# Hybrid encoder trunk: the seams between stages, the order of cross attention, and chunk attention's transposes and first scores between the products of v

## The reference

```python
mem_n = rms_norm(mem, mem_norm_g)                       # 256 memory rows
for layer in range(2):
    if layer == 0:   # S5 heads and gated DeltaNet heads, then one output projection "abo"
        x = x + concat([a_out, b_out]) @ ab_w_out
    else:            # 16 heads of 64; a chunk of 64 sees itself and 8 chunks back, with a bias
        q, k, v = split(rms_norm(x, c_norm_g) @ c_w_qkv) ; q, k = rms_norm(q), rms_norm(k)
        x = x + (softmax(q @ k.T * scale + bias) @ v) @ c_w_out
    # cross attention, 4 heads of 256, into the 256 memory rows
    q = rms_norm(rms_norm(x, xa_norm_g) @ w_q) ; k, v = split(mem_n @ w_kv) ; k = rms_norm(k)
    x = x + (softmax(q @ k.T / 16) @ v) @ w_out
    h = rms_norm(x, f_norm_g)
    x = x + (silu(h @ w_gate) * (h @ w_up)) @ w_down    # 2816 hidden
```

## Time and profile before

| | |
|---|---|
| median of 3 runs | 1712.14 us (1711.04 to 1712.47) |
| the profiled execution | 1712.62 us, its span 1710.8 us |
| PE busy | 1644.2 us, 96% of the span |
| DVE, ACT, POOL busy | 766.8, 627.0, 228.7 us |
| TensorE clock granted, mean | 0.99 |

### The profile page before, as it was taken

The page is one execution under the profiler, slowest core; times in us unless marked ns, Lnnn a source line. Parts: engine busy times, 40 slices in busy tenths (PEclk is TensorE's granted clock), DMA queues, the critical chain, the costliest instruction groups (busy, mean ns, idle before and its releaser), DMA issues.

```text
span 1710.8 us, 22110 instructions
## 1 busy us (share of the span) xinstructions
PE 1644.2 (96%) x9102; PEld 1337.5 (78%) x9102; DVE 766.8 (45%) x996; ACT 627.0 (37%) x1022; POOL 228.7 (13%) x309
## 2 busy tenths in 40 slices
PE   5999999899899999999999998899989999999999
PEld 4788787778678888888888885588767788888887
DVE  4669345544524444442244438734353444444222
ACT  6543433444515222221133336824451422222110
POOL 3863233010001111110000000000000011111000
PEclk9998999999999999999999998999999999999999
DMA  6612012242022333332222321225302143333221
GB/s 204 134 50 74 2 53 75 86 161 98 30 69 74 98 98 98 98 98 98 99 87 86 99 99 50 75 74 169 102 25 75 53 119 95 94 92 95 92 98 74
DMA packets 146799, 151.82 MB, mean 89 GB/s; under 512 B 8864, under 2 KB 109344, under 8 KB 146592
## 3 DMA queue, kind: packets, MB, share of 16 engines
q1 hardware_dynamic: 146720, 150.69, 29.0%
HBM read 147.53 MB, written 3.15 MB: 88 GB/s over the span
## 4 chain that ended last, share of the span: by engine, by line
PE 91%; DVE 4%; ACT 3%; issue 1%; DMA 0%; POOL 0%; SPq 0%; ACTq 0%; DVEq 0%
PE ps L325 25%; PE ps L327 25%; PE ps L326 25%; PE ps L1679 2%; PE ps L1656 1%; PE ps L2016 1%; PE ps L2028 1%; PE ps L959 1%; PE ps L2038 1%; PE ps L417 1%; PE ps L1274 1%; PE ps L889 1%; ACT w_hi L293 1%; PE ps L1079 1%; PE ps L1363 1%
## 5 line engine op out<-in xcount | busy, mean ns | idle before, releaser
L325 PE MATMUL ps<-h_hi,w_hi 128*128 128x512 f32 x864 | 338.1, 391 | 4.2 <-DVE w_lo L1849 3.9
L326 PE MATMUL ps<-h_lo,w_hi 128*128 128x512 f32 x864 | 336.7, 390 | 0.0
L297 DVE TENSOR_TENSOR w_lo<-raw,w_hi 128x2048 fp32r<-128x2048 f32 x70 | 160.5, 2292 | 389.8 <-ACT w_hi L293 389.8
L293 ACT ACTIVATE w_hi<-raw 128x2048 fp32r<-128x2048 f32 x84 | 160.8, 1916 | 423.6 <-PE ps L327 423.0
L327 PE MATMUL ps<-h_hi,w_lo 128*128 128x512 f32 x704 | 274.4, 390 | 0.0
L325 PEld LDWEIGHTS ps<-h_hi,w_hi 128*128 128x128 f32 x864 | 162.6, 188 | 38.8 <-issue 5.3
L326 PEld LDWEIGHTS ps<-h_lo,w_hi 128*128 128x128 f32 x864 | 162.7, 188 | 33.3
L1849 DVE TENSOR_TENSOR w_lo<-raw,w_hi 128x2048 fp32r<-128x2048 f32 x44 | 138.1, 3139 | 53.5 <-ACT w_hi L1831 53.5
L327 PEld LDWEIGHTS ps<-h_hi,w_lo 128*128 128x128 f32 x704 | 132.5, 188 | 27.8
L1831 ACT ACTIVATE w_hi<-raw 128x2048 fp32r<-128x2048 f32 x44 | 84.3, 1916 | 161.1 <-PE ps L327 161.1
L325 PE MATMUL ps<-w_hi,a_hi 128*128 128x512 f32 x352 | 137.3, 390 | 1.7 <-DVE up L1847 1.7
(11 more groups left out here) (372 smaller groups left out, 2639.2 us busy)
## 6 DMA issues: line engine op xcount, KB each, us to landing
raw<-in_f_w_gate SPq DMA_DIRECT2D x44, 512.0 KB, 4.0
raw<-in_f_w_up SPq DMA_DIRECT2D x44, 512.0 KB, 5.2
raw<-in_f_w_down SPq DMA_DIRECT2D x44, 512.0 KB, 4.4
raw<-in_xa_w_kv SPq DMA_DIRECT2D x16, 1024.0 KB, 5.0
raw<-in_c_w_qkv SPq DMA_DIRECT2D x12, 1024.0 KB, 5.1
raw<-in_ab_w_in SPq DMA_DIRECT2D x10, 1024.0 KB, 5.9
raw<-in_xa_w_q SPq DMA_DIRECT2D x8, 1024.0 KB, 5.0
raw<-in_xa_w_out SPq DMA_DIRECT2D x8, 1024.0 KB, 5.0
```

The costliest lines, as they stand in the source:

```text
L293: a.activation(w_hi[:, n % 2, :], raw[n % 2], ACT.Copy).then_inc(sem("w_hi"), 1)
L297: v.tensor_tensor(w_lo(n)[:, n % 2, :], raw[n % 2], w_hi[:, n % 2, :].bitcast(F32), ALU.subtract).then_inc(sem("w_lo"), 1)
L325: pe.matmul(out, a[0], b[0], start=start, stop=False)
L326: pe.matmul(out, a[0], b[1], start=False, stop=False)
```

## The change

- The normalised memory's transposes move between the two halves of abo1. They use four banks for the eight blocks (`norm_bank`), so a block of 256 columns shares a bank with another; ACT writes the second four after DVE has done with the first. PE then waits for all eight low parts and goes on to kv without waiting for the last additions to x.
- The first four transposed blocks of x move between the halves of kv's last projection, the other four between the halves of xq's first; ACT and DVE write them there.
- Cross attention: ACT loads the table of the exponential ahead of k's blocks; PE transposes q's blocks 0 to 3, does head 0's scores, transposes blocks 4 to 7, does head 1's scores. Head 0's scores wait for k's and for q's first two blocks alone. DVE rescales a head before it takes the maxima of a later one.
- FFN up: the first turn of ACT's and DVE's loops is written out, with the weights of block 2 split ahead of SiLU and of the gated product.
- Chunk attention: v's first projection has q's and k's 16 transposed blocks between its tiles (banks 4 to 7), v's second the scores of pairs 0 and 1 (banks 0 to 3). ACT and DVE write the blocks, v's rows and the first exponentials between pieces; piece ca4_1 moves behind k's last row tile and piece cao0_1 into the turn m = 6. The probabilities of pairs 0 and 1 lie elsewhere in memory.

The diff, cut to its core:

```diff
+        def norm_bank(n, k):
+            banks = KT * n // TT
+            return ps[:, k % banks, k // banks * n * P:(k // banks + 1) * n * P]
...
-        def rows_pe(pe, t, name, srcT, tiles, bank, ready=None, bank_free=None, between=None, mid=None):
+        def rows_pe(pe, t, name, srcT, tiles, bank, ready=None, bank_free=None, between=None, mid=None, step=None):
...
+                    if step is not None:
+                        step(kh, i)
...
+            def x_between():
+                pe.wait_ge(sem(f"{t}_k"), after(f"{t}_k", 4))
+                turn_rows_pe(pe, f"x{l}", 0, "co_x" if l else "mo_x")
...
+            pe.wait_ge(sem(f"{t}_q"), after(f"{t}_q", 8))
+            xq_turn_pe(pe, l, range(0, 4))
...
+            exp_table(a)
             kv_turned_act(a, l)
...
             maxes(0)
+            xq_turned_dve(v, l, (5, 7))
+            rescale(0)
             maxes(1)
-            rescale(0)
             turned(0)
...
                     turned(h + 1)
-                if h + 3 < XH:
-                    maxes(h + 3)
                 if h + 2 < XH:
                     rescale(h + 2)
                 out_lo(h)
+                if h + 3 < XH:
+                    maxes(h + 3)
...
             xa_scores_pe(pe, l, 0)
+            xq_turn_pe(pe, l, range(4, KT))
             xa_scores_pe(pe, l, 1)
...
+            weights_hi(0, 0)
+            silu(0, 0)
+            silu(0, 1)
+            weights_hi(0, 1)
+            with a.Fori(1, FT // 2) as j:
...
+            gate(0, 0)
+            weights_lo(0, 0)
+            gated(0, 0)
+            gate(0, 1)
+            gated(0, 1)
+            weights_lo(0, 1)
+            with v.Fori(1, FT // 2) as j:
...
+                        step={4: step_turn, 5: step_scores}.get(p))
+        CA_TURNS = ((), range(0, 3), range(3, 6), range(6, 8), range(8, 10), range(10, 12), range(12, 14), range(14, 16))
+        CA_FIRST = ((), ((0, CA_ROWS[0:3]),), ((0, CA_ROWS[3:4]),), (), ((1, CA_ROWS[0:3]),), ((1, CA_ROWS[3:4]),), (), ())
...
+            pieces_hi(a, "ca4_1")
+            for t in (0, 2, 4):
+                ca_turned(a, t)
+            pieces_hi(a, "ca5_0")
+            for t, values in ((6, ()), (8, (16,)), (10, (17,)), (12, (18, 19)), (14, ())):
+                ca_turned(a, t)
+                for n in values:
+                    ca_value_rows(a, n)
+            pieces_hi(a, "ca5_1")
+            pieces_hi(a, "ca5_1", 1)
+            a.wait_ge(sem("c_max"), 1)
+            for e in range(2):
+                for i in CA_EXP:
+                    ca_exp(a, 0, e, i)
+            for n in range(20, 24):
+                ca_value_rows(a, n)
...
+            if t < 4:
+                pe.wait_ge(sem("c_rows"), 13 + t)
+            else:
+                pe.wait_ge(sem(f"c_T{'av'[t % 2]}"), after(f"c_T{'av'[t % 2]}", (t - 4) // 2 + 1))
...
-            ca_scores_pe(pe, 0)
-            ca_scores_pe(pe, 1)
+            pe.wait_ge(sem("c_v"), 8)
...
+                if m == CH // 2 - 2:
+                    pieces_hi(a, "ca5_1", 2)
...
-            rows_pe(pe, "mo", "abo1", cat, TT, 4)
-            pe.wait_ge(sem("mo_x"), after("mo_x", 8))
-            norm_pe(pe, "m", mem_x, mem_x)
+            rows_pe(pe, "mo", "abo1", cat, TT, 4, between=mem_between)
+            ready_T(pe, "m", KT - 1)
```

More of the change, by code:

```diff
@@ L438, in sqrt_table, with exp_table @@
             a.wait_ge(sem("act_warm"), count[name])
+        def exp_table(a):
+            a.activation(warm, pcol("one"), ACT.Exp).then_inc(sem("act_warm"), 1)
+            name = "act_warm"
+            count[name] = count.get(name, 0) + 1
+            a.wait_ge(sem("act_warm"), count[name])
         def squares_act(a, t, x, junk, dst, ready=None, halves=(0, 1)):
@@ L1626, in xq_act @@
                 a.wait_ge(sem(f"{t}_turned"), after(f"{t}_turned", k + 1))
-                a.activation(qT[:, k, :], ps[:, (k + 4) % 8, :], ACT.Copy, scale=pcol(f"xq_g{l}", 0)).then_inc(sem(f"{t}_qTa"), 1)
+                a.activation(qT[:, k, :], ps[:, 4 + k % 4, :], ACT.Copy, scale=pcol(f"xq_g{l}", 0)).then_inc(sem(f"{t}_qTa"), 1)
         def xq_dve(v, l):
@@ L1649, in xa_scores_pe @@
             if h < 2:
-                for k in range(6) if h == 0 else range(6, KT):
+                if h == 0:
+                    pe.wait_ge(sem(f"kv{l}_kTa"), after(f"kv{l}_kTa", 4))
+                    pe.wait_ge(sem(f"kv{l}_kTv"), after(f"kv{l}_kTv", 4))
+                for k in (2 * h, 2 * h + 1):
                     pe.wait_ge(sem(f"xq{l}_qT{'av'[k % 2]}"), after(f"xq{l}_qT{'av'[k % 2]}", k // 2 + 1))
@@ L1662, in xa_turn_pe @@
             pe.wait_ge(sem(f"{t}_p"), after(f"{t}_p", h + 1))
+            if h == 0:
+                for e in "av":
+                    pe.wait_ge(sem(f"xq{l}_qT{e}"), after(f"xq{l}_qT{e}", 4))
             if h > 0:
@@ L1940, in bank_free, with turned_free, step_turn, step_scores @@
                     pe.wait_ge(sem("c_rows"), n - 7)
+            def turned_free(n):
+                for t in range(n - 8, n - 7):
+                    pe.wait_ge(sem(f"c_T{'av'[t % 2]}"), after(f"c_T{'av'[t % 2]}", t // 2 + 1))
+            def step_turn(kh, i):
+                for t in CA_TURNS[4 * kh + i]:
+                    ca_turn_pe(pe, t)
+            def step_scores(kh, i):
+                for m, rows in CA_FIRST[4 * kh + i]:
+                    ca_scores_pe(pe, m, rows)
             for p in range(6):
@@ L2086, in exp @@
             def exp(m, e, i):
-                p = p_c(m, e, i)
-                a.activation(p, p, ACT.Exp, bias=c_neg[:, m % 2, e, i:i + 1], accum_out=c_sum[:, m % 2, e, i:i + 1]).then_inc(sem("c_exp"), 1)
-            a.wait_ge(sem("c_max"), 1)
-            for e in range(2):
-                for i in CA_EXP:
-                    exp(0, e, i)
+                if (m, e) != (1, 0):
+                    ca_exp(a, m, e, i)
             for m in range(CH // 2):
@@ L2285, in _ @@
                 kv_pe(pe, l)
-                pe.wait_ge(sem(f"kv{l}_k"), after(f"kv{l}_k", 4))
-                pe.wait_ge(sem(f"kv{l}_v"), after(f"kv{l}_v", 4))
-                for half in range(2):
-                    turn_rows_pe(pe, f"x{l}", half, "co_x" if l else "mo_x")
                 xq_pe(pe, l)
@@ L2376, in _ @@
                 pieces_hi(a, f"kv{l}3_1", 2)
-                for half in range(2):
-                    turned_hi_act(a, f"x{l}", f"xa_g{l}", half)
+                turned_hi_act(a, f"x{l}", f"xa_g{l}", 1)
                 xq_act(a, l)
@@ L2460, in _ @@
                 kv_dve(v, l)
+                turned_lo_dve(v, f"x{l}", f"xa_g{l}", 0)
                 pieces_lo(v, f"kv{l}3_1", 2)
-                for half in range(2):
-                    turned_lo_dve(v, f"x{l}", f"xa_g{l}", half)
+                turned_lo_dve(v, f"x{l}", f"xa_g{l}", 1)
                 xq_dve(v, l)
```

179 lines of the change are left out of this document (104 added, 75 removed).

## The result

The median after the change is 1683.12 us (1680.52 to 1684.19, 4 runs), beside 1711.59 us (1710.72 to 1712.47, 4 runs) of the kernel before: ratio 0.9831, 95% interval 0.9814 to 0.9848, 28.5 us less. The prediction was 1681.5 us. The profiled execution took 1684.19 us, with a span of 1682.4.

What follows compares the result with a forecast made beforehand. PE, busy 96% of the span, was taken to bound the kernel, so only its standing or slow running could be won. Terms 3.7 + 3.5 + 8.8 + 4.8 + 9.8 = 30.6 us gave 1681.5 us, range 1675 to 1690.

Steps and rivals of the forecast that it cites:

- the likeliest case: Whole kernel: the forecast's own sum holds, 1681.5 us, with a range of 1676 to 1687 and a chance of 0.60.
- A, memory's seam: Layer 0, abo1 to kv: moving memory's transposes between abo1's halves removes PE's standing around them, saving 3.7 us.
- B, x's seam: kv and xq, both layers: x's transposes between projection halves leave 0.4 us of standing, saving 1.75 us a layer, 3.5 in all.
- C, cross attention: Both layers: rescaling waits and a clock fall go, two new waits come; 7.4 becomes 3.05 us, saving 4.4 a layer, 8.8 in all.
- D, FFN's start: Start of FFN up, both layers: earlier split shortens PE's wait for block 2's low part to 0.45 us, saving 4.8 us.
- E, chunk attention: Transposes and first scores between v's products win 11.4 us, less 1.6 for the moved piece: 9.8 us saved.
- the last values start 1.6 us later: End of chunk attention's loop: piece cao0_1 in turn m = 6 delays DVE's copy of the last pair's probabilities, costing 1.6 us.
- in turns 0 to 5 the piece would have been hidden: Chunk attention's loop: piece cao0_1 would be covered in turns 0 to 5, but nothing covers it in turn m = 6.
- wait for evacuations in v's first projection: Rival, chunk attention: PE stands for every pair because blocks are written out late, 8 us, giving 1689.5; chance 0.17.
- The seams' waits: Rival: standing removed in A, B and D returns at the next piece, losing 12.0 us, giving 1693.5; chance 0.05.
- The clock kept falling: Rival: clock falls behind remaining waits in cross attention, FFN and the loop's start, 5.4 us in all, giving 1687; chance 0.15.
- The slower case: Rival: transposes between v's products keep the clock at half there, 35 us for 192 matmuls, giving 1716.5; chance 0.03.

Runs made afterwards that it cites:

- Experiment 11: Kernel after the change, with x's second four blocks transposed behind the second tile of xq's first half: 1682.5 us.
- Experiment 2: Kernel after the change, with cross attention's order put back as before: 1695.94 us.
- Experiment 5: Kernel after the change, with ACT's and DVE's halves of piece cao0_1 moved behind the loop of chunk attention: 1680.47 us.
- experiment 7: Kernel after the change, with piece cao0_1 in turn m = 2 instead of 6 on both engines: 1683.52 us.
- experiments 3 and 4: Kernel after the change with one part put back each: 3, the start of FFN up, 1688.21 us; 4, memory's and x's transposes, 1690.15 us.
- experiment 10: Kernel after the change, with DVE's low part of the next weights piece in cross attention moved from head 0 to head 2: 1682.12 us.
- experiment 9: Kernel after the change, without the early load of the exponential's table in cross attention: 1685.33 us.
- experiment 1: Kernel after the change, with chunk attention put back as before: 1689.58 us.
- experiments 7 and 8: Kernel after the change: 7, piece cao0_1 in turn 2, 1683.52 us; 8, exponential's table loaded behind ACT's first two blocks of q, 1682.12 us.

## Why the prediction was right

The time came out at 1683.1 us for 1681.5, within the likeliest case's own range. In the touched stretches 29.8 us were won for 30.6 forecast; the mixer gave 1.3 back. Four of the five terms came out within 0.7 us, the fifth 2.3 too large. C and D gave 1.4 us more than forecast, which hides part of what E gave less: that the sum is 0.8 off is in part luck.

- **A, memory's seam:** 3.3 us at abo and 0.44 in kv, 3.8 for 3.7. The wait left ahead of kv's second piece, forecast 0.5, is 0.54: the chain of addition, square and two halves of the piece was counted right.
- **B, x's seam:** 1.77 and 1.72 for 1.75 a layer (from kv's first product to k's transposes 94.09 and 93.03 us before, 91.88 and 91.31 after, the 0.44 of A taken off in layer 0). Experiment 11 shows the remaining 0.51 us to be what it was said to be, a chain without cover.
- **C, cross attention:** what A and B leave of the stretches, 4.7 us a layer (6.95 - 1.77 - 0.44, and 6.45 - 1.72), for 4.4. The four waits left are 1.17, 0.35, 0.25 and 1.31, together 3.08 for 3.05. So the misfit is in what was removed: some 7.8 for 7.4. Experiment 2 puts C back as a whole; what the order of DVE's list and the scores between q's blocks are worth singly is not shown.
- **D, FFN's start:** 5.5 for 4.8. The forecast had PE 0.45 us late for the gated product; it is about 0.1.
- **E, chunk attention:** 7.5 for 9.8. The main part held. v's two projections run from 968.77 to 1025.55 in the trace of after, 56.8 us, for 43.5 of products, 7.0 of transposes and 5.6 of scores, 56.1: nothing waits there, and 0.7 us goes at the changes between products and the rest: 0.3 in the part with the blocks (29.0 us for 64 transposes and 96 matmuls), 0.4 in that with the scores (22.3 us for 32 and 72). The loop starts 0.94 us behind them, for 0.9. The step that failed is the tail, "the last values start 1.6 us later": they do, but then the clock falls and they take 4.02 us instead of 2.37, so the tail costs 3.2 us. 0.7 and 1.6 are the whole 2.3 us. Experiment 5 prices the two apart: 1.7 for the piece, 1.65 for the fall.
- The step "in turns 0 to 5 the piece would have been hidden" was wrong, though nothing in the sum hung on it: experiment 7.

**The rivals.** PE did not wait for evacuations in v's first projection (busy 55.32 of 55.32 us). The seams' waits were not passed on: the two stretches that follow one with moved work and hold none themselves (chunk attention's output projection, layer 1's FFN down) have the same length as before within 0.03 us, A, B and D came out at their size or above it, and experiments 3 and 4 give them back. The clock kept falling in one place, not in those named: not in cross attention (clock 1.00 over both stretches), not at FFN's start, but at the end of the loop, where no fall had been forecast (six of the eight runs of that code have one there, experiment 10). The slower case did not come: 64 transposes and 32 scores lie between v's products at a granted clock of 1.00. The Trainium skill ("TensorE: Matmul & The Clock Gate", section "Part 4: PE-mode transpose") would have the full clock not engage for transposes; neither those 64 nor the ones in the earlier trace rows bear this out. Nor do the rows show the drain of 1380 ns that the Trainium skill ("ScalarE: Activation LUTs", section "What ACT_TABLE_LOAD costs") adds to a switch of tables: in experiment 9 the load has 1.28 us with 0.02 and 0.01 us around it.

**What in it was chance.** Of the 30.6 us, about 7 were half clock in the one profile of before: 1.3 in each layer's cross attention, 1.5 in FFN, and the 2.9 of chunk attention that experiment 1 takes out. The forecast took each fall of that execution as its full price. Experiments 1 to 3 show that in the same code a fall stays out behind a wait of 2.50 us and comes twice for once behind waits of 2.66. What decides a single fall stays open: the runs show one behind waits of 0.65 us (experiment 5) and none behind 1.27 (experiment 7). The total was not chance to the same degree. The 27 executions of the kernel before that ran beside the experiments have a mean granted clock of 0.987 to 0.993, median 0.989; the profiled one has 0.990, and the four of the kernel after 0.995 to 0.997. So the one trace held about as much half clock as a usual execution of the kernel before, which the forecast could not know from it, and in each execution of the kernel after more than half of it is gone.

## What to carry to other kernels

On an engine that is busy 96% of the time, list the places where it stands and price each from the rows on both sides, with the new waits that the move leaves; here four of five terms came out within 0.7 us of their forecast. Before work is moved into a loop for cover, take the busy time that its engine already has in one turn: with 7.7 of 8.1 us taken, neither turn that was tried covered 2.3 us. A fall of the clock behind a wait is a price with a chance: compare the stretch in two executions before it goes into a sum. And look at what it falls on: behind the last wait it cost 1.65 us, one pair earlier, ahead of that wait, nothing.

## What the runs showed of the hardware

- The granted clock falls to half at different places in executions of the same code. The mixer, untouched, had 6.8, 10.2 or 13.65 us at half and took 284.5 to 288.6 us with that; a fall turned up at the head of abo in experiments 7 and 8 (that stretch 51.6 us instead of 50.0) and in the mixer in experiment 11 (291.5 us).
- 12 transposes and the 12 matmuls of products behind them take 4.08 to 4.09 us in the kernel after, where 0.109 and 0.227 us for each make 4.03; 8 transposes and 12 matmuls take 3.61 for 3.60. A group of transposes among products cost 0.01 to 0.06 us there beyond its own time.
- DVE's low part (128x2048) takes 2.29 us, and 3.42 where POOL's subtraction (128x512) starts 0.01 to 0.02 us before it; where DVE starts first, POOL's takes 3.42 us instead of 1.29 (start of FFN up in the kernel before and in experiment 3).
